# Product-key expert layer: 24 of 128 tiles of V loaded once for all tokens and multiplied by a matrix of gated activations, their gathers left out by index

## The reference, cut to what matters

```python
def peer_ffn(hn, w_pq, sub_keys, u_tab, v_tab):       # K = 16, 8 heads, 128 keys per half
    q = (xt @ w_pq).reshape(T, PEER_HEADS, 2, PEER_D_KEY // 2)
    s = jnp.einsum('thpd,hpkd->thpk', q, sub_keys)
    top_s, top_i = lax.top_k(s, K)
    cand = top_s[:, :, 0, :, None] + top_s[:, :, 1, None, :]
    best_s, best_c = lax.top_k(cand.reshape(T, PEER_HEADS, K * K), K)
    ia = jnp.take_along_axis(top_i[:, :, 0], best_c // K, axis=-1)
    ib = jnp.take_along_axis(top_i[:, :, 1], best_c % K, axis=-1)
    expert = ia * PEER_N_KEYS + ib                     # 0 .. 16383
    gate = jax.nn.softmax(best_s, axis=-1)
    a = jnp.einsum('td,ted->te', xb, u_tab[eb])        # per block of 128 tokens
    hidden = gb * jax.nn.gelu(a)
    return jnp.einsum('te,ted->td', hidden, v_tab[eb])
```

## Time and profile before

| | us |
|---|---|
| median of 3 runs | 3222.11 |
| profiled execution: time / span of its instructions | 3215.15 / 3213.0 |
| first gather issued (span's start = 0) | 1900.7 |
| last row added to the output | 3202.4 |
| PE, DVE, ACT, POOL busy in the whole span | 2578.5, 2057.8, 1040.6, 916.7 |
| bytes moved by DMA in the whole span | 862.14 MB |

### The profile page before, as it was taken

One profiled execution on the slowest core, in us unless ns is written; L12 is line 12 of the kernel. 1 busy time (PEld: TensorE's weight loads), 2 busy tenths in 40 slices (PEclk: granted clock), 3 DMA queues, 4 the chain that ended last, 5 costly groups with the idle time before them and its releaser, 6 DMA issues.

```text
span 3213.0 us, 32168 instructions
## 1 busy us (share of the span) xinstructions
PE 2578.5 (80%) x11258; PEld 1879.9 (59%) x11258; DVE 2057.8 (64%) x2782; ACT 1040.6 (32%) x1685; POOL 916.7 (29%) x534
## 2 busy tenths in 40 slices
PE   8999989999999999999989873666656555565665
PEld 7888778888878879898778771222222222222222
DVE  5586655555555545365545689777777777776665
ACT  5454655555543335355655530000000000000000
POOL 0011000000000000000000027677777776676653
PEclk9999999999999999899999996777787777777777
DMA  6444545555555555444334359999999999999997
GB/s 254 143 160 155 184 156 185 192 186 190 189 183 178 189 183 177 142 173 144 144 120 169 144 193 392 422 421 422 421 422 422 421 421 422 422 422 421 422 422 306
DMA packets 118820, 862.14 MB, mean 268 GB/s; under 512 B 13336, under 2 KB 13352, under 8 KB 14768
## 3 DMA queue, kind: packets, MB, share of 16 engines
q0 software_dynamic: 74784, 544.79, 40.9%
q1 hardware_dynamic: 43776, 313.73, 27.3%
q10 hardware_dynamic: 144, 2.10, 0.2%
HBM read 858.44 MB, written 4.22 MB: 268 GB/s over the span
## 4 chain that ended last, share of the span: by engine, by line
DMA 16%; PE 15%; DVE 12%; POOL 10%; issue 3%; ACT 2%; DVEq 0%; ACTq 0%; POOLq 0%
DMA rows<-peer_v,arena 16%; POOL rows L1165 10%; PE ps L540 10%; DVE arena L2212 3%; PE ps L1102 2%; DVE XR L2215 2%; DVE arena L170 1%; DVE arena L163 1%; DVE WL L454 1%; DVE arena L164 0%; DVE arena L167 0%; DVE arena L160 0%; DVE arena L2187 0%; DVE arena L2189 0%; DVE arena L2190 0%
## 5 line engine op out<-in xcount | busy, mean ns | idle before, releaser
L1102 PE MATMUL ps<-rows,rstd 128*128 128x512 f32 x1256 | 751.0, 762 | 526.4 <-DMA rows<-peer_v,arena 375.4
L454 DVE SCALAR_TENSOR_TENSOR WL<-ring,PA,WH 128x512 fp32r<-128x512 f32 x896 | 632.2, 752 | 473.5 <-ACT WH L437 458.1
L1102 PEld LDWEIGHTS ps<-rows,rstd 128*128 128x128 f32 x1256 | 300.4, 248 | 976.4 <-issue 520.8
L2212 DVE CUSTOM_DVE_ANT_0 arena<-rows,arena 128x2048 f32<-128x2048 f32 x256 | 586.9, 2293 | 276.0 <-DMA rows<-peer_u,arena 251.9
L1165 POOL DMA_INDIRECT rows<-peer_u,arena x256 | 457.3, 1786 | 284.9 <-DVE arena L2212 109.3
L436 ACT ACTIVATE WH<-ring,PA 128x512 fp32r<-128x512 f32 x448 | 324.0, 723 | 541.7 <-PE ps L540 390.0
L1165 POOL DMA_INDIRECT rows<-peer_v,arena x256 | 426.1, 1665 | 205.5 <-PE ps L1102 139.0
L540 PE MATMUL ps<-WH,HH 128*128 128x512 f32 x1120 | 442.3, 395 | 9.4 <-DVE WL L454 7.0
L540 PE MATMUL ps<-WH,HL 128*128 128x512 f32 x1120 | 437.8, 391 | 0.0
L540 PE MATMUL ps<-WL,HH 128*128 128x512 f32 x1120 | 437.4, 391 | 0.0
L540 PE MATMUL ps<-HH,WH 128*128 128x256 f32 x1088 | 312.5, 287 | 23.0 <-DVE WL L454 23.0
(11 more groups left out here) (335 smaller groups left out, 2966.4 us busy)
## 6 DMA issues: line engine op xcount, KB each, us to landing
ring<-stream SPq DMA_DIRECT2D x292, 1024.0 KB, 4.8
rows<-peer_u,arena POOLq DMA_INDIRECT x256, 20.2
rows<-peer_v,arena POOLq DMA_INDIRECT x256, 22.6
arena<-xT SPq DMA_DIRECT2D x4, 512.0 KB, 8.9
bias_rows<-bias_scratch POOLq DMA_DIRECT2D x1, 2048.0 KB, 13.7
arena<-xT ACTq DMA_DIRECT2D x1, 2048.0 KB, 10.4
arena<-memT POOLq DMA_DIRECT2D x1, 2048.0 KB, 9.1
out<-arena SPq DMA_DIRECT2D x2, 1024.0 KB, 7.1
```

What stands on the lines that cost most here:

```text
L454: ins = nc.vector.scalar_tensor_tensor(out=half_tile(WL, u)[:, s], in0=raw_half(u)[:, s], scalar=gain[d], in1=half_tile(WH, u).bitcast(f32 ...
L1102: last = mm(ps[:, 4 * (g // PEER_H) + q, :], DIAG[:, k % DIAGS, :], rows[:, n % ROWS, q * CH:(q + 1) * CH], start=g % PEER_H == 0 and j == ...
L2212: ins = V.tensor_tensor_reduce(out=JUNK, in0=rows[:, n % ROWS, :], in1=HN[:, tt, :], scale=1.0, scalar=0.0, op0=ALU.mult, op1=ALU.add, acc ...
```

## The change

Expert tiles c = 0 to 23 are the 24 x 128 rows of V with ia = c. Each of them is now loaded once, as a plain DMA of 1 MB with the 128 rows ib = 0 to 127 on the partitions ("dense"), and is multiplied on TensorE for both tiles of tokens by a matrix DENSE_H[tt][:, c, :] (ib x token) that holds hidden where the token picked expert (c, ib), and zero elsewhere. Eight matmuls of 512 columns per tile c.

- A second list IDV has for each pick the expert's number, plus 16384 where ia < 24; V is gathered by IDV. The coefficient of the gathered row is zero there (`finish` writes it into GA by one more instruction). A skipped row leaves what lay in the slot.
- DENSE_H is built by token: `turn_ids` transposes ia, ib and hidden of a tile on TensorE (three transposes). In eight batches of 16 tokens VectorE writes a matrix of ia == c times hidden (2 instructions of 384 columns) and 16 one-hot matrices of ib (4 instructions of 512 columns), TensorE multiplies them (16 matmuls of 24 columns), ScalarE copies the result to DENSE_H. Tile 0's batches lie in groups 9 to 12, tile 1's in the first 30 V rows after the last U row.
- The order is new. In groups 1 to 15, 9 V rows stand among 16 U rows (135 in all, all by TensorE). After the last U row stand the other 121 V rows, m = 0 to 120; from m = 33 to 107 the 24 dense tiles lie between them, one for 3.2 rows. There TensorE takes m % 8 in (2, 5, 7) for m < 34, every sixth for m < 108, every second up to m = 118; VectorE takes the rest. The list is 536 long, before it was 512.
- `add_sum(0)` runs twice: after the last U row, and after the last dense tile, when the squares and the norm of tile 0 follow.

```diff
-def by_matmul(g, j):
-
-    return j % 2 == 0 and j < 14 if g == GROUPS - 1 else j % 8 in (0, 1, 3, 4, 6)
+N_DENSE = 24
+LEAD = 9
+BATCH = 16
+BATCHES = P // BATCH
+DENSE_FROM, DENSE_STEP = 34, 3.2
+V_ORDER = [(g, j) for g in range(GROUPS) for j in range(PEER_K)]
+N_LEAD = LEAD * (GROUPS - 1)
+N_LAST = len(V_ORDER) - N_LEAD
+def by_matmul(m):
+    if m < 0:
+        return True
+    if m < DENSE_FROM:
+        return m % 8 in (2, 5, 7)
+    if m < N_LAST - 13:
+        return m % 6 == 0
+    return m % 2 == 0 and m < N_LAST - 2
 ROW_ORDER = []
-for _g in range(GROUPS + 1):
+_v = 0
+for _g in range(GROUPS):
     for _j in range(PEER_K):
-        if _g < GROUPS:
-            ROW_ORDER.append(("u", _g, _j))
-        if _g:
-            ROW_ORDER.append(("v", _g - 1, _j))
+        ROW_ORDER.append(("u", _g, _j))
+        if _g and LEAD * _j // PEER_K != LEAD * (_j + 1) // PEER_K:
+            ROW_ORDER.append(("v", *V_ORDER[_v]))
+            _v += 1
...
+ROW_LAST = len(ROW_ORDER)
+_d = 0
+for _m in range(N_LAST):
+    ROW_ORDER.append(("v", *V_ORDER[N_LEAD + _m]))
+    while _d < N_DENSE and _m + 1 >= DENSE_FROM + DENSE_STEP * _d:
+        ROW_ORDER.append(("dense", _d, 0))
+        _d += 1
...
 ROW_AT = {row: n for n, row in enumerate(ROW_ORDER)}
 ROW_DONE = []
 _count = {"dve": 0, "pe": 0}
 for _tab, _g, _j in ROW_ORDER:
-    _by = "pe" if _tab == "v" and by_matmul(_g, _j) else "dve"
+    _by = "pe" if _tab == "dense" or _tab == "v" and by_matmul(PEER_K * _g + _j - N_LEAD) else "dve"
     _count[_by] += 1
     ROW_DONE.append((_by, _count[_by]))
+BATCH_AT = {}
+for _b in range(BATCHES):
+    BATCH_AT[ROW_AT["u", 9 + _b // 2, 3 + 8 * (_b % 2)]] = (0, _b)
+    BATCH_AT[ROW_AT["v", *V_ORDER[N_LEAD + 4 * _b + 1]]] = (1, _b)
+TURN_AT = {ROW_AT["u", 8, 3]: 0, ROW_LAST: 1}
+KEEP_AT = {n + 3: b for n, b in BATCH_AT.items()}
+LAST_DENSE = ROW_AT["dense", N_DENSE - 1, 0]
...
+        DENSE_H = [take(0, N_DENSE, P)[0], take(10 * 1024, N_DENSE, P)[0]]
+        ONE_HOT, _ = take(3072, 8, P)
+        IA_GATE, _ = take(13312, 2, BATCH, N_DENSE)
...
+            def turn_ids(tt):
+                pe.wait_ge(sem("hidden"), PEER_H * (tt + 1))
+                if tt:
+                    pe.wait_ge(sem("first_sum"), 1)
+                for k, v in enumerate((IAF, IBF, HI)):
+                    last = nc.tensor.transpose(ps[:, (6, 2)[tt], k * P:(k + 1) * P], v[:, tt, :], ident)
+                last.then_inc(sem("transposes"), 1)
+            def dense_gates(tt, b):
+                n = BATCHES * tt + b
+                if n >= 2:
+                    pe.wait_ge(sem("dense_h_kept"), n - 1)
+                for q in range(4):
+                    pe.wait_ge(sem("one_hots"), 4 * n + q + 1)
+                    for k in range(4):
+                        last = mm(ps[:, (4, 0)[tt] + b % 2, (4 * q + k) * N_DENSE:(4 * q + k + 1) * N_DENSE], ONE_HOT[:, 4 * (q % 2) + k, :],
+                                  IA_GATE[:, n % 2, 4 * q + k, :], start=True, stop=True)
+                    last.then_inc(sem("dense_h"), 1)
+            def dense_rows(n, c):
+                pe.wait_ge(sem(f"row_in{n % ROWS}"), 16 * (n // ROWS + 1))
+                pe.wait_ge(sem("dense_h_kept"), TT * BATCHES)
+                for tt in range(TT):
+                    for q in range(4):
+                        last = mm(ps[:, 4 * tt + q, :], DENSE_H[tt][:, c, :], rows[:, n % ROWS, q * CH:(q + 1) * CH],
+                                  start=tt == 0 and c == 0, stop=tt == 0 and c == N_DENSE - 1)
+                last.then_inc(sem("rows_pe"), 1)
+            def gathered_rows(n, g, k):
+                pe.wait_ge(sem(f"row_in{n % ROWS}"), 16 * (n // ROWS + 1))
+                pe.wait_ge(sem("diagonals"), k + 1)
+                tt = g // PEER_H
+                mine = [r for r, (tab, h, j) in enumerate(ROW_ORDER) if tab == "v" and h // PEER_H == tt and ROW_DONE[r][0] == "pe"]
+                for q in range(4):
+                    last = mm(ps[:, 4 * tt + q, :], DIAG[:, k % DIAGS, :], rows[:, n % ROWS, q * CH:(q + 1) * CH],
+                              start=n == mine[0], stop=n == mine[-1])
+                last.then_inc(sem("rows_pe"), 1)
             pe.wait_ge(sem("scores_kept"), 8)
...
-            for g in range(GROUPS):
-                if g:
-                    k = diagonals(g - 1, k)
-                if g + EARLY < GROUPS:
+            for n, (tab, g, j) in enumerate(ROW_ORDER):
+                if n in KEEP_AT:
+                    keep_dense_h(*KEEP_AT[n])
+                if tab == "u" and j == 12 and g + EARLY < GROUPS:
                     gate(g + EARLY)
-                act.wait_ge(sem("peer_poly"), g + 1)
-                ch.mark(A(PO, PO, ACT.Tanh, scale=math.sqrt(2 / math.pi)), "peer_tanh")
-                if g == PEER_H + 1:
+                if tab == "v" and ROW_DONE[n][0] == "pe":
+                    diagonal(g, j, k)
+                    k += 1
+                if tab == "u" and j == PEER_K - 1:
+                    act.wait_ge(sem("peer_poly"), g + 1)
+                    ch.mark(A(PO, PO, ACT.Tanh, scale=math.sqrt(2 / math.pi)), "peer_tanh")
+                if n == LAST_DENSE + 4:
...
-                    ch.link(V.tensor_reduce(XS[:, part, :], EQ, X, ALU.add))
-                ch.link(V.scalar_tensor_tensor(out=ID, in0=XS[:, 0, :], scalar=float(PEER_KEYS), in1=XS[:, 1, :],
-                                               op0=ALU.mult, op1=ALU.add))
+                    ch.link(V.tensor_reduce((IAF, IBF)[part][:, tt, es], EQ, X, ALU.add))
+                ia, ib = IAF[:, tt, es], IBF[:, tt, es]
+                ch.post(V.scalar_tensor_tensor(out=ID, in0=ia, scalar=float(PEER_KEYS), in1=ib, op0=ALU.mult, op1=ALU.add))
+                ch.post(V.tensor_scalar(SKIP, ia, float(N_DENSE), float(PEER_KEYS * PEER_KEYS), ALU.is_lt, ALU.mult))
+                ch.join()
+                ch.link(V.tensor_tensor(SKIP, SKIP, ID, ALU.add))
+                ch.link(V.tensor_copy(IDV[:, tt * PEER_E + 16 * h:tt * PEER_E + 16 * h + 16], SKIP))
...
+                gathered = GA[:, tt, 16 * h:16 * h + 16]
+                ch.link(V.scalar_tensor_tensor(out=x, in0=x, scalar=RC, in1=gathered, op0=ALU.mult, op1=ALU.mult))
+                ch.mark(V.scalar_tensor_tensor(out=gathered, in0=IAF[:, tt, 16 * h:16 * h + 16], scalar=float(N_DENSE), in1=x,
+                                               op0=ALU.is_ge, op1=ALU.mult), "hidden")
+            def add_sum(tt, done, read):
+                dve.wait_ge(sem("rows_pe"), read)
...
+            def one_hots(tt, b):
+                n = BATCHES * tt + b
+                if b == 0:
+                    dve.wait_ge(sem("transposes"), 15 + tt)
+                    ch.link(V.tensor_copy(IDS_T.rearrange("p a b -> p (a b)"), ps[:, (6, 2)[tt], 0:3 * P]))
+                if n >= 2:
+                    dve.wait_ge(sem("dense_h"), 4 * (n - 1))
+                ia, ib, hid = (IDS_T[:, k, b * BATCH:(b + 1) * BATCH].rearrange("p (t a) -> p t a", a=1) for k in range(3))
+                v = IA_GATE[:, n % 2, :, :]
+                ch.link(V.tensor_tensor(v, ia.to_broadcast([P, BATCH, N_DENSE]),
+                                        IOTA[:, 0:N_DENSE].rearrange("p (a k) -> p a k", a=1).to_broadcast([P, BATCH, N_DENSE]), ALU.is_equal))
+                ch.link(V.tensor_tensor(v, v, hid.to_broadcast([P, BATCH, N_DENSE]), ALU.mult))
+                for q in range(4):
+                    if 4 * n + q >= 2:
+                        dve.wait_ge(sem("dense_h"), 4 * n + q - 1)
+                    ch.mark(V.tensor_tensor(ONE_HOT[:, 4 * (q % 2):4 * (q % 2) + 4, :], ib[:, 4 * q:4 * q + 4, :].to_broadcast([P, 4, P]),
+                                            IOTA.rearrange("p (a k) -> p a k", a=1).to_broadcast([P, 4, P]), ALU.is_equal), "one_hots")
...
+                if n == ROW_LAST:
+                    finish(GROUPS - 1, done)
+                    add_sum(0, done, ROW_DONE[ROW_AT["v", PEER_H - 1, PEER_K - 1]][1])
+                    dve.sem_inc(sem("first_sum"), 1)
+                if n in BATCH_AT:
+                    one_hots(*BATCH_AT[n])
+                if n == LAST_DENSE + 3:
+                    add_sum(0, done, ROW_DONE[LAST_DENSE][1])
+                    dve.sem_inc(sem("sum_ready"), 1)
+                if n == LAST_DENSE + 8:
+                    dve.wait_ge(sem("gfin_in"), 16)
+                    last_norm(0)
+                if n == len(ROW_ORDER) - 1:
+                    add_sum(1, done, _count["pe"])
+                if ROW_DONE[n][0] == "pe":
+                    continue
+                done = dve_row(tab, g, j)
+                if tab == "u":
                     if g and j == 0:
                         finish(g - 1, done)
-                    if g and not by_matmul(g - 1, j):
-                        done = dve_row("v", g - 1, j)
                     if j == 7 and g + EARLY < GROUPS:
                         dve.wait_ge(sem("rows_dve"), done)
                         choose(g + EARLY)
```

(61 more changed lines are left out.)

34 lines of the change are left out of this document (18 added, 16 removed).

## The result

The changed kernel takes 3237.40 us (median of five runs, 3231.77 to 3238.02), the kernel before 3222.86 beside it (3217.92 to 3224.88). The ratio is 1.0042, with a 95% interval of 1.0027 to 1.0056: slower, where 3196 us and faster were forecast. The profiled execution has a span of 3235.5 us.

A forecast was written before the change was run, and what follows sets the result against it. Gathers at 422 GB/s bound the stage until the last U row, then VectorE and TensorE: 937.5 + 101.8 + 213.3 + 23 = 1275.6 us, plus 10.6, from 1900.7 gives a 3186.9 span, median 3196 us; range 3165 to 3238.

The forecast's parts named there:

- The hand-over of the batches: Behind the last U row, VectorE and TensorE share two buffers: 6 us per batch, 48 us for eight.
- 101.8: Us from the last U row to the dense tiles: VectorE's V rows, eight batches and the copy (87 to 131).
- The batches beside the U rows: Tile 0's batches in groups 9 to 12: VectorE up to 17 us late, hidden by gathers in flight, priced 0.
- The cover: Beside the U rows, gathers land 20.2 us after issue, so DMA has work while VectorE is under 20 us late.
- 937.5: Us from first issue to the last lead row's landing: 23.2 start, 3 catching up, 636.9 U and 274.4 V transfers.
- rival 1: V gathers: skips fall unevenly on 16 DMA engines and the fullest sets the pace; +28 us, 3224; chance 0.26.
- 233.9: Us for the dense stretch: TensorE's 213.3 plus 23 for the last 13 rows, less the last row's 2.4.
- a dip behind the last U row: DMA rate falls for some 40 us there, VectorE over nine tenths busy, POOL waiting for slots.
- Rival 2: Whole stage: transfers stay the bound, batches at 4.1 us, slots never fill; 3167 us; chance 0.12; its sign, no dip.
- Rival 3: V gathers: skipped indices are transferred after all, so 24 MB are added; 3288 us; no saving, chance 0.07; sign, packets as before.
- its own last sign: Last U row to the end: the forecast is wrong if this stretch is not 338 us, within 15.
- its stretch of 213.3 us: TensorE from the dense tiles on: 165.1 us for 24 tiles plus 48.2 for 14 V rows, at 2.4 GHz.

The follow-up runs named there:

- oh16: The changed kernel with 16 one-hot matrices instead of 8, so VectorE can write a whole batch ahead of TensorE: 3207.21 us, ratio 0.9958 to the kernel before.
- no_batches: The changed kernel without the batches and transposes of either tile, dense tiles multiplied by whatever lies in that memory: 3194.72 us, ratio 0.9912 to the kernel before.
- no_batches1: The changed kernel without tile 1's transposes and eight batches, dense tiles using tile 0's matrix twice: 3206.28 us, ratio 0.9942 to the kernel before.
- oh16_spread: The changed kernel with 16 one-hot matrices and 24 of 128 rows of every V gather skipped, spread over partitions: 3196.13 us, ratio 0.9908 to the kernel before.
- after_spread: The changed kernel with 6144 skipped V rows spread by a rotating mask instead of following ia < 24: 3217.89 us, ratio 0.9987 to the kernel before.
- skip_natural: The kernel before with the 6066 V picks of ia < 24 skipped, no dense tiles or batches: 3144.60 us, ratio 0.9751.
- skip_spread: The kernel before with 6144 V rows skipped, in three rotating residues of the partition, no dense tiles or batches: 3117.25 us, ratio 0.9664.
- skip_fixed: The kernel before with 6144 V rows skipped, always those of partitions 0 to 23, no dense tiles or batches: 3210.02 us, ratio 0.9957.

## Why the prediction was wrong

Its sum failed in three terms, all too low. The stage took 1325.3 us where 1286.2 stood (1275.6 + 10.6), 39.1 more: 13.1 up to the last U row, 20.2 from there to the first dense product, 7.0 in the dense stretch, and 1.2 less at the end. The other 2.3 of the 41.4 us by which the median missed lie before the stage and around the span.

- **The hand-over of the batches, the step that failed most.** "They hand over through two buffers; a batch costs VectorE at least 4.1 and at most the sum, 9.6. I take 6, nearer to overlap." Behind VectorE's last batch only "the copy on ScalarE 1.5" stood. From the last U row to the first dense product it took 122.0 us, where 101.8 stood. VectorE's timeline splits both:

```
us                                           forecast   changed kernel   oh16
last U row to the first batch                     7.5              9.7    9.7
eight batches                                    48.0             58.5   36.9
18 V rows between them                           44.8             43.0   43.0
end of the last batch to the dense product        1.5             10.8   11.4
```

  The 9.7 hold the U row itself, 2.3 us, where the forecast counted from its landing. A batch cost VectorE 7.3 us on average (5.0 to 9.2), and 4.6 with 16 buffers. What was left out is that TensorE works in order and has one or two V rows of 3.4 to 6.8 us each before a batch, which is as long as a batch, so that VectorE can't be ahead by more than half a batch. The last term was missed for the same reason. TensorE still has the last batch to do, and then two V rows that stand ahead of the first dense tile; the copy lies beside them. The chain that ended last (start, us, what; the third line is the first dense tile):

```profile
2967.45 6.99 PE ps L1151 x32
2974.45 8.48 PE ps L1170 x16
2982.93 6.87 PE ps L1160 x16
```

  So 10.5 of the 20.2 us are the batches and 9.3 the end behind them. That `oh16` takes 100.9 us there, next to the 101.8 of the forecast, is luck: its batches are 11 us cheaper than priced, and its end is 10 us longer.
- **The batches beside the U rows**, "priced 0; without the cover 17 us". The cover, 20 us of gathers in flight, did not hide them: `no_batches` is 11.6 us faster than `no_batches1`, and `oh16` 7.6 us shorter there. The last U row came at 950.6, not 937.5.
- **The uneven skips**, rival 1, at a chance of 0.26. It is true, and costs 20 us (priced 28); the sum of the forecast had nothing for it. Of these 10.2 lie beside the U rows and 10.2 in the dense stretch, which took 240.9 us from the first dense product, not 233.9. The argument "nothing in the trace says which packet goes where" should have lowered no chance: 16 completion packets in each of 512 gathers pointed to a gather that is dealt out to all 16 engines, and any fixed way of dealing makes skips uneven.
- **Perhaps the two share one cover.** Beside the U rows, over the 936.8 us of `oh16_spread`, the shallow buffers alone cost 3.6 us (`after_spread`, 940.4), the uneven skips alone 6.2 (`oh16`, 943.0), and both together 13.8 (950.6). If one cover has to hide both, that is what it would look like. But the 4 us between the sum and the two together rest on marks of one profiled execution each, and the timed runs do not bear them out, so this is not shown.
- **Right:** the bytes (down 49.7 MB in gathers), a dip behind the last U row, 1.00 of clock in the dense stretch, POOL's issues hidden, TensorE nearly full in the dense stretch. Rival 2 is out by the dip. Rival 3 is out by the bytes, though its sign, packets that do not fall, is what the trace shows: the sign was badly chosen. By its own last sign the forecast is wrong: from the last U row's start to the last row's end it is 365 us, not 338 within 15. One sum is slightly off and decides nothing: at 1.2 GHz its stretch of 213.3 us would take 213 us more, not 205.

The sum from the other side, in medians: the skips alone in the order of before, -80 (`skip_natural`); 24 dense tiles of 2.488 us, +60, worked out and not run by itself; that makes -20, where `no_batches` measured -29 against its own before (the 9 between them stay open). The batches of tile 0 add 12 and those of tile 1 add 31: -29 + 12 + 31 = +14. (This closes on the changed kernel's 14.5 by construction, since the 12 and the 31 are differences to it.) So the saving was real, three quarters of it were spent on the dense loads, and the batches took more than the rest. The range reached to 3238 and held the time by 0.6 us, which is luck: that end was there for rival 1 alone, at 28 us, and the batches made up the larger part. The sign was wrong.

## What to carry to other kernels

Leaving out single rows of a gather saves what the fullest DMA engine saves, so count the rows per engine before counting bytes, and read the rate: the busy share stays near 1. Two in-order engines that hand over through a few buffers take the price of overlap only if the buffers cover the longest piece of other work that the consumer has between two hand-overs; otherwise take a price near the sum. What the consumer has to do in order between the last hand-over and the work that waits for it is a term of its own. And a stretch that comes out as forecast shows little until its terms do.

## What the hardware showed

- A row left out by its index still is a packet: 4 bytes, 9 ns (an 8 KB one has a median of 313 ns). Gathers keep 144 packets each.
- With uneven skips some 8 KB packets take longer: the 99th percentile from 2100 to 2800 us is 322 ns before, 333 in `skip_spread`, 485 in the changed kernel, 535 in `skip_natural`, 777 in `skip_fixed`. This lifts the DMA share, so it reads 0.95 to 1.01 while the rate is down by up to 9%.
- POOL issues a plain 1 MB load in 0.59 us, a gather in 0.99 when it need not wait.
- A gap of 4.8 us on TensorE was followed by a batch at nearly twice the time (6.88 us at a granted clock of 0.51, for 3.78 us at 1.00). The same batches took 3.78 and 3.81 us where TensorE came from V rows without a gap at the high clock, and 3.65 in `oh16` in the same place.
